# Compression products of an attention layer in another form and order, and an output projection that takes its input tile by tile

## What is computed

```python
def compress_blocks(kv, pe, w1, w2):
    sub = kv[:, :n_sub * CMP_STRIDE].reshape(b, n_sub, CMP_STRIDE, g, dh)
    pe = pe.reshape(2, CMP_STRIDE, 1, dh)
    w1 = w1.reshape(2, CMP_STRIDE, dh, CMP_HIDDEN)
    first = jnp.einsum('bnsgd,sdh->bngh', sub + pe[0], w1[0])
    second = jnp.einsum('bnsgd,sdh->bngh', sub + pe[1], w1[1])
    hid = jax.nn.silu(first[:, :-1] + second[:, 1:])
    return hid @ w2
```

## Time and profile before

| | us |
|---|---|
| median of 3 runs | 1764.48 |
| lowest and highest run | 1758.5, 1765.56 |
| the profiled run | 1756.73 |
| its span, first to last instruction | 1755.1 |
| TensorE busy | 1592.0 (91%) |
| VectorE, ScalarE, GpSimd busy | 913.7, 746.8, 190.0 |
| mean granted clock of TensorE | 0.93 |
| DMA, mean over the span | 119 GB/s |

### The profile page before, as it was taken

How to read it: one execution, slowest core, us unless ns; L and a number is a source line. 1 busy time by engine, 2 the same in 40 slices (tenths; PEclk the granted TensorE clock), 3 DMA queues, 4 the chain that set the end, 5 groups by cost and what they waited for, 6 DMA issues and landing times. The chain is left out here.

```text
span 1755.1 us, 37259 instructions
## 1 busy us (share of the span) xinstructions
PE 1592.0 (91%) x13470; PEld 1318.9 (75%) x13470; DVE 913.7 (52%) x1741; ACT 746.8 (43%) x1504; POOL 190.0 (11%) x396
## 2 busy tenths in 40 slices
PE   6999989999999999899999999978767777999897
PEld 6999756556556655569999999966555557999897
DVE  5775134443434444364677744323555654777732
ACT  5675233453344334353454533223454544544522
POOL 1331001021101201100000000031211100000000
PEclk7999969999989999979999999966999887999999
DMA  7444331321331332145555757463443513555650
GB/s 176 146 144 154 125 103 40 96 84 40 88 89 51 79 90 70 55 107 145 145 144 144 184 133 172 136 200 108 147 139 120 166 48 97 148 150 151 167 132 31
DMA packets 283163, 208.13 MB, mean 119 GB/s; under 512 B 29103, under 2 KB 274895, under 8 KB 282592
## 3 DMA queue, kind: packets, MB, share of 16 engines
q1 hardware_dynamic: 273750, 174.22, 35.7%
q0 software_dynamic: 9248, 31.80, 5.9%
q10 hardware_dynamic: 42, 0.44, 0.1%
HBM read 183.57 MB, written 22.85 MB: 118 GB/s over the span
## 5 line engine op out<-in xcount | busy, mean ns | idle before, releaser
L621 PE MATMUL psum<-h_rounded,weights_low 128*128 128x320 f32 x1248 | 391.4, 314 | 0.0
L623 PE MATMUL psum<-h_rounded,weights_high 128*128 128x320 f32 x1248 | 386.7, 310 | 0.0
L622 PE MATMUL psum<-weighted_x_low,weights_high 128*128 128x320 f32 x864 | 266.3, 308 | 0.0
L1082 PE MATMUL psum<-sbuf_resident 128*128 128x504 f32 x512 | 251.8, 607 | 0.0
L621 PEld LDWEIGHTS psum<-h_rounded,weights_low 128*128 128x128 f32 x1248 | 235.1, 188 | 3.0 <-DVE weighted_x_low L488 0.5
L623 PEld LDWEIGHTS psum<-h_rounded,weights_high 128*128 128x128 f32 x1248 | 234.7, 188 | 0.0
L597 DVE TENSOR_TENSOR weights_low<-sbuf_resident,weights_high 128x2048 fp32r<-128x2048 f32 x90 | 205.7, 2287 | 50.9 <-ACT weights_high L582 50.9
L582 ACT CAST weights_high<-sbuf_resident 128x2048 fp32r<-128x2048 f32 x90 | 169.9, 1893 | 91.7 <-PE psum L623 69.7
L622 PEld LDWEIGHTS psum<-weighted_x_low,weights_high 128*128 128x128 f32 x864 | 165.3, 191 | 0.2
L1115 ACT COPY sbuf_resident<-psum 64x256 f32<-64x256 f32 x256 | 93.8, 366 | 135.5 <-PE psum L1075 132.9
L696 DVE SCALAR_TENSOR_TENSOR sbuf_stages<-sbuf_stages,sbuf_resident 128x344 f32<-128x344 f32 (+1 forms) x184 | 105.5, 574 | 56.4 <-ACT sbuf_stages L678 52.6
(11 more groups left out here) (429 smaller groups left out, 2795.5 us busy)
## 6 DMA issues: line engine op xcount, KB each, us to landing
sbuf_resident<-in_ffn_w_up_dram SPq DMA_DIRECT2D x88, 512.0 KB, 5.0
sbuf_resident<-in_gdn_w_in_dram SPq DMA_DIRECT2D x48, 512.0 KB, 4.6
sbuf_resident<-in_ffn_w_down_dram SPq DMA_DIRECT2D x32, 704.0 KB, 6.0
sbuf_resident<-in_cache_nsa_kv_dram SPq DMA_DIRECT2D x256, 64.0 KB
sbuf_stages<-in_state_gdn_s_dram POOLq DMA_DIRECT2D x16, 512.0 KB, 5.7
out_gdn_s_sample_dram<-sbuf_stages SPq DMA_DIRECT2D x16, 512.0 KB, 3.7
sbuf_resident<-in_gdn_w_out_dram SPq DMA_DIRECT2D x16, 512.0 KB, 5.5
sbuf_stages<-in_cache_nsa_kv_dram POOLq DMA_DIRECT2D x64, 128.0 KB, 3.4
```

Source lines behind the costliest of these rows:

```text
L621: pe.matmul(out, w_lo, x_hi_tile, start=first, stop=False)
L622: pe.matmul(out, w_hi, x_lo_tile, start=False, stop=False)
L623: return pe.matmul(out, w_hi, x_hi_tile, start=False, stop=last)
L1082: last = pe.matmul(psum[:, H_BANK[t], 0:4 * NC2], w1[:, v, 8 * half + m, t * P:(t + 1) * P], blocks, start=(m == 0 and half == 0), stop=(m ...
```

## The change

The first weights of the compression (keys) are loaded by GpSimd in the projection, into the space of the rows that are written later; the second in the rows stage, ahead of the compressed cache. Each half has its own semaphore. In the rows stage the copies into `sub` come first on both engines. TensorE then multiplies the keys' part at once, ahead of the turns, with the operands exchanged: `sub` (64 or 63 columns) is stationary, 256 columns of weights stream past, and the two halves of the sum go to the two halves of PSUM's partitions, in turn. ScalarE copies the result to SBUF (`z_rows`), and four matmuls with the identity add the two halves and turn them. The values' part comes after the gates. In the output projection ScalarE rounds the first weights first, and the input is rounded and split in 8 tiles, which TensorE's first unit takes one by one.

```diff
-                  ("nsa_in", KD), ("nsa_out", 1),
+                  ("nsa_in", KD), ("nsa_out", KD),
...
+            def load_w1_again(pool, v):
+                pool.dma_start(w1_again[v], ins["nsa_cmp_w1"][0, v].rearrange("s d h -> (s d) h").rearrange("(c p) h -> p c h", p=P)).then_inc(w1_again_in[v], 16)
...  pool_in, after the load of w2
+                load_w1_again(pool, 0)
                 pool.wait_ge(gate_split, 1)
...
+            rows_at = after_rows_s - NKV * KV_DIM
-            w1_again = [space.take(16, CHID, off=ring_at + 2 * SLOT), space.take(16, CHID)]
+            w1_again = [space.take(16, CHID, off=rows_at), space.take(16, CHID)]
+            z_rows = space.take(2, CHID, off=xpg_at + 2 * 2 * 4 * PCMP)
...  pe_rows
+                def hidden_rows(kv, name):
+                    pe.wait_ge(w1_again_in[kv], 16)
+                    for m in range(8):
+                        for half in range(2):
+                            last = pe.matmul(psum[64 * half:64 * half + 64 - half, 6 + kv, 0:CHID], sub[:, kv, m, half:4 * PSUB],
+                                             w1_again[kv][:, 8 * half + m, :], start=(m == 0), stop=(m == 7))
+                    last.then_inc(pe_steps.sem, pe_steps.step(name))
+                def hidden_columns(kv, rows_name, name):
+                    pe.wait_ge(act_steps.sem, act_steps.count(rows_name))
+                    for t in range(2):
+                        for half in range(2):
+                            pick = ident[:, 64 * half:64 * half + 64].rearrange("p (x n) -> p x n", x=4)[:, :, 0:PCMP]
+                            last = pe.matmul(psum[:, 6 + kv, CHID + t * 60:CHID + (t + 1) * 60], z_rows[:, kv, t * P:(t + 1) * P], pick,
+                                             start=(half == 0), stop=(half == 1))
+                    last.then_inc(pe_steps.sem, pe_steps.step(name))
+                pe.wait_ge(dve_steps.sem, dve_steps.count("sub7"))
+                pe.wait_ge(act_steps.sem, act_steps.count("sub7"))
+                hidden_rows(0, "zk")
                 for n, (tb, rows, q) in enumerate(groups):
...
+                hidden_columns(0, "zk", "hk")
                 pe.wait_ge(dve_steps.sem, dve_steps.count("gate"))
...
-                pe.wait_ge(w1_again_in, 32)
-                pe.wait_ge(dve_steps.sem, dve_steps.count("sub7"))
-                pe.wait_ge(act_steps.sem, act_steps.count("sub7"))
-                for kv, name in enumerate(("hk", "hv")):
-                    for t in range(2):
-                        blocks = lambda m, half: sub[:, kv, m, :].rearrange("p (x n) -> p x n", x=4)[:, :, half:half + PCMP]
-                        last = hidden_products_again(pe, kv, t, psum[:, 6 + kv, t * 60:(t + 1) * 60], blocks)
-                    last.then_inc(pe_steps.sem, pe_steps.step(name))
+                hidden_rows(1, "zv")
+                hidden_columns(1, "zv", "hv")
+                pe.wait_ge(act_steps.sem, act_steps.count("g7"))
                 pe.wait_ge(act_steps.sem, act_steps.count("hk"))
...  act_rows: its order now
+                sub_copies(act, "act")
+                act.wait_ge(gate_scaled, 1)
+                act.activation(gates48, gates48, ACT.Exp, scale=-1.0).then_inc(act_steps.sem, act_steps.step("gexp"))
+                copy_hidden_rows(0, "zk")
...  then the odd row groups
+                silu_rows(0, "hk")
+                copy_hidden_rows(1, "zv")
+                silu_rows(1, "hv")
...  dve_rows: memset of z_rows, sub_copies, den, gate, then the even row groups; the rest as it was
+                dve.memset(z_rows[64:P], 0.0).then_inc(dve_steps.sem, dve_steps.step("zero"))
+                sub_copies(dve, "dve")
...  pool_rows
+                load_w1_again(pool, 1)
                 pool.dma_start(ckT, ck_dram).then_inc(cmp_in, 16)
                 pool.dma_start(cv, cv_dram).then_inc(cmp_in, 16)
-                for v in range(2):
-                    pool.dma_start(w1_again[v], ...).then_inc(w1_again_in, 16)
...  act_out
-                act.copy(out_hi, hT).then_inc(x_hi, 1)
-                for n in range(4):
+                high_part(act, "nsa_out", 0, 0, KD * 2)
+                for k in range(KD):
+                    act.copy(out_hi[:, k, :], hT[:, k, :]).then_inc(x_hi, 1)
+                for n in range(1, 4):
                     high_part(act, "nsa_out", 0, n, KD * 2)
...  pe_out
-                pe.wait_ge(x_lo, split_count("nsa_out"))
                 for n in range(4):
-                    multiply_unit(pe, "nsa_out", 0, n, pair_tile, lambda k: out_hi[:, k, :], lambda k: out_lo[:, k, :], KD)
+                    multiply_unit(pe, "nsa_out", 0, n, pair_tile, lambda k: out_hi[:, k, :], lambda k: out_lo[:, k, :], KD,
+                                  from_tile=0 if n == 0 else None)
...  dve_out
-                dve.wait_ge(x_hi, split_count("nsa_out"))
-                dve.tensor_tensor(out_lo, hT, out_hi, ALU.subtract).then_inc(x_lo, 1)
+                for k in range(KD):
+                    dve.wait_ge(x_hi, SPLITS["nsa_out"][0] + k + 1)
+                    dve.tensor_tensor(out_lo[:, k, :], hT[:, k, :], out_hi[:, k, :], ALU.subtract).then_inc(x_lo, 1)
```

50 lines of the change are left out of this document (23 added, 27 removed).

## The result

| | us |
|---|---|
| before, median (lowest to highest) | 1764.48 (1758.5 to 1765.56) |
| after, median (lowest to highest) | 1748.06 (1743.14 to 1754.09) |
| after over before | 0.9913, 95% interval 0.9884 to 0.9941 |
| the profiled run after, its span | 1743.14, 1741.5 |
| mean granted clock of TensorE after | 0.935 |

What follows compares the result with a forecast made beforehand. TensorE was taken to set the pace over most of the span. Gains of 18.5 (rows stage) and 4.5 (output projection) less 0.5 (loop) made 22.5 us, forecasting 1742.0 us, range 1733 to 1752.

Steps and rivals of the forecast that it cites:

- Projection: Projection stage: the moved 2 MB load costs 0 to 0.7 us, taken as 0; up to 6 without cover.
- 5.3 spare: Projection: unit 3's weights would be ready at 1088.9, its products start at 1094.2, leaving 5.3 us of cover.
- Compression products: Rows stage: 32 records per half at 0.107 us full clock; first half 5.4 us, second 3.4.
- TensorE's chain: Rows stage: TensorE's own work would alone open the loop at 1173.8, before GpSimd is done.
- GpSimd's chain: Rows stage: 15.5 us from last row copy to last load issued, ending last at 1176.9; stage gain 18.5 us.
- Out-projection: Start of the output projection: TensorE begins at 1462.6, not 1467.1; 4.5 us gained, bounds 2.8 and 5.2.
- rival 5: Several stages: more than forecast, from cheaper records, quicker keys and better clock; gain 27, 1737 us; chance 0.06.
- Loop: Loop: same computation, but clock dips may move in its first pass; 0 to 3 us lost, 0.5 taken.
- rival 4: Loop: clock returns later in every pass, up to 1838 us; chance 0.03 slower, 0.08 within 0.5%.
- Rival 1: Rows stage: half clock throughout, products 6.8 us and turns 8.3; gain 16.1, 1748.4 us; chance 0.18.
- Rival 2: Rows stage: products don't run in pairs, first half 8.7 us; gain 19.2, 1745 us; chance 0.08.
- rival 3: Rows stage: keys land 8.7 us after issue, not 3.4; gain 17, 1747 us; chance 0.07.

Runs made afterwards that it cites:

- fill: Changed kernel plus 12 useless identity products on TensorE, filling its idle time before the wait for the copies into sub; 1741.95 us.
- after_again: The changed kernel unaltered, run once more for a second profile; 1760.33 us.
- rows_only: Changed kernel with the output projection's lines put back as before; 1749.36 us, ratio 0.9927 against the kernel before.
- w1_late: Changed kernel with the keys' 2 MB of weights asked for only after six units of the projection; 1741.37 us.
- late_keys_no_drain_fill: Changed kernel with late keys' weights, key loads before the wait for row copies, no GpSimd drain, and 12 filling products; 1735.45 us, ratio 0.9848 against the kernel before.
- apart: Changed kernel with each weight half multiplied as 8 products into the lower partitions, then 8 into the upper; 1757.82 us.
- late_and_keys: Changed kernel with keys' weights asked for after six projection units and key loads ahead of the wait for row copies; 1733.67 us, ratio 0.9818 against the kernel before.

## Why the prediction came out as it did

The time, 1748.06, lies in the range (1733 to 1752) and on the side forecast, 6.1 us above the forecast. Two terms of the sum failed, both on the side of too much gain: a delay was bounded by the bytes at peak rate, and a cover was counted without the drain, though its row stood in the trace of before. That the time is in the range all the same is owed to the range's width, which was made for the rivals and the clock and not for these two.

- **Projection, 0 forecast, 4.7 in the profile, a mean of 3.0 over eight traces: wrong.** The failed step is "6.0 us, the most that it can delay another load". That divides the new bytes by the peak rate. Unit 3's weights came 7.4 us late, past the 5.3 spare. In the 16 us in question the engines were full (DMA share 1.08, 0.75 before) and moved 330 GB/s, not 352; with the 2 MB in the air beside them, SyncE's four loads of 256 KB took a median of 10.6 us, 7.5 before. The sign that was named for being wrong, idle TensorE near 1094, is there. "If that cover were gone it would be up to 6" was the right size for a cost put at zero. The Trainium skill (DMA: Bandwidth & Descriptors, Queues, rings and completion order) says that each DMA engine goes round the queues that have work, one packet at a time. The trace agrees as far as it goes: q0 sent 784 packets of some 5 KB beside 7328 packets of 570 bytes on q1, and both made progress at once; no run here varied the packets.
- **Compression products: right.** First products 3.64 us after the opening (3.5 forecast); first half 5.01 (5.4; bounds 3.4 and 6.8 hold all of 3.69 to 6.64); a record at full clock 0.115 (0.107, from L1097's 0.118 and L1058's 0.088: the nearer row alone would have been better). The half clock behind idle TensorE was forecast and is shown by fill. The 36 turns took 4.15 us at 1.00, and the last row copy ended at 13.4 (13.8). The second half took 5.37 us where 3.4 at full clock were forecast; 3.69 is what eight of the eleven paired traces have. GpSimd's chain covered it here.
- **TensorE's chain** ended 25.4 us after the opening, 26.2 forecast: right, and not the last, as forecast.
- **GpSimd's chain: right that it is last, wrong in size.** From the last row copy to the last issue's end 17.1 us, 15.5 forecast: the read of the page numbers left GpSimd idle for 5.32 us, 3.83 before. It is 5.2 to 5.4 in all seven traces with the changed order and late keys; in after the first two of the eight reads take 1.39 and 0.88 us instead of 0.51 and 0.30, and the reason is open. Then the drain, which had no term: 4.7 us from there, 3.8 net of the keys' own landing. "So GpSimd, which was covered by 29 us" is the step that failed: it counted the chain to the last issue and not to what the barrier waits for, the drain's end at 1178.3, 19 us ahead. Stage gain 14.2 for 18.5.
- **Out-projection, 4.5 forecast: right at its start, too small in all.** 4.4 at its start and 1.2 in the rest, 5.6 together, over the upper bound of 5.2. The forecast said that the stretch at half clock "only moves"; it became shorter, 5.2 us of products before and 3.3 after, worth some 1.0. That early return of the clock is a part of rival 5.
- **Loop, 0.5 forecast, 2.6 in the profile: not to be told from the clock's variation**, which is 12 us for one program. My allowance of 3 us for the phase was far too small for one execution; the median of the runs tames it. The sign named for rival 4, passes longer than 31 us, tells nothing: after has passes of up to 32.9 behind the first, but before has one of 31.7 too.

Sum against sum: 22.5 - 4.7 (projection) - 4.3 (rows) - 2.1 (loop) + 1.1 (out-projection and rest) + 1.0 (ahead of t0) = 13.5, the 13.6 of the spans. One profile is one execution; means are nearer to the median of the runs. The rows stage is 36.7 on average in the four traces that have it as in the change (after, after_again, rows_only, w1_late), a gain of 13.2 and so 5.3 under the forecast. With that, the projection's mean of 3.0 and the out-projection's 1.1 above its term, the forecast would have been 22.5 - 3.0 - 5.3 + 1.1 = 15.3, beside a measured 15.4 (10.4 to 20.5). That is a check of the size and not a proof.

**Rivals.** Rival 1 (half clock through the stage, 1748.4) gives the measured number and is wrong all the same: the clock came back inside the first products, and the turns ran at 1.00. By the rule of the Trainium skill that stood behind it (TensorE: Matmul & The Clock Gate, Part 4: PE-mode transpose), the turns would have pulled the clock down; this trace has 40 records at 1.00 behind a short dense stretch, so it does not agree. In eight of the eleven paired traces the clock is still at 1.00 in the second half, behind the turns and the small products; in after, fill and late_keys_no_drain_fill it falls there. Rival 2 fell with apart, rival 3 with the keys' landing at 2.5 us, which is rival 5's figure. Rival 4 isn't supported: TensorE enters the loop from ten idle microseconds, and the loop's length varies by more between two executions of one program (262.9 and 275.0) than between before and after. Rival 5's cheaper records didn't come.

## What to carry over

A stage's end is what its barrier waits for: follow each engine to the end of its drain, and read how long that drain lasts in the trace even where it is hidden, because a transfer issued last that nobody wants yet becomes the whole core's wait once the cover goes. A load that is moved into a stretch where the DMA engines are already busy delays the urgent ones by more than its bytes at peak rate; where it isn't needed for another 80 us, put it behind the stage's tight start (here 3.0 us on average for moving one line). Compare stages and not single times: one program's 262.9 and 275.0 us for the same loop are larger than most of the effects looked for.

## What was not expected of the hardware

- GpSimd's drain lasts until the transfers it has issued have landed: 11.1 us with a last landing after 10.1 (before), 5.5 with one after 4.4 (after), and 7.1 in late_and_keys, where it ends 1.0 us behind the landing of the last store.
- 24 products of no use in TensorE's idle time kept the granted clock at 1.00 and made the next 32 records 1.3 to 2.9 us shorter; the half clock came later instead, and the next 32 of their kind took 5.37 and 6.32 us, 3.69 in most other traces.
- Products with 64 columns of weights each, into alternate halves of the output partitions, take 0.115 us for 256 columns of data; one half after the other, 0.22 from start to start at a granted clock of 1.00.
- Products of 128 x 128 by 320 start 148.9 ns apart in some stretches and 146.7 in others, at the same granted clock of 1.00; the reason is open.
- The granted clock's mean over one stage of the same program was 0.84 and 0.78 in two executions, 12 us of 263.
